# Down projection's last classic part: tokens on the output partitions, with the order of loads, copies and squares changed

## What is computed

```python
def swiglu(h, w_gate_up, w_down):
    gu = h @ w_gate_up
    g, u = gu[..., :D_FF], gu[..., D_FF:]
    return (jax.nn.silu(g) * u) @ w_down
...
        h = h + swiglu(rms_norm(h, g_ffn[l]), w_gate_up[l], w_down[l])
    return rms_norm(h, g_final)
```

## Time and profile before

| | |
|---|---|
| median of 3 runs | 2607.68 us (2606.93 to 2610.78) |
| the profiled execution | 2607.0 us |
| its span, first to last instruction | 2605.2 us |
| mean granted TensorE clock | 0.999 |
| TensorE busy | 2587.1 us, 99% of the span |
| VectorE busy | 2042.0 us, 78% |
| ScalarE busy | 1329.1 us, 51% |
| chain that ended last, by engine | TensorE 98%, VectorE 1% |

### The profile page before, as it was taken

The page is one execution under the profiler, slowest core; times in us unless marked ns, Lnnn a source line. Parts: engine busy times, 40 slices in busy tenths (PEclk is TensorE's granted clock), DMA queues, the critical chain, the costliest instruction groups (busy, mean ns, idle before and its releaser), DMA issues.

```text
span 2605.2 us, 36741 instructions
## 1 busy us (share of the span) xinstructions
PE 2587.1 (99%) x13665; PEld 2228.5 (86%) x13665; DVE 2042.0 (78%) x3366; ACT 1329.1 (51%) x2465; POOL 96.7 (4%) x154
## 2 busy tenths in 40 slices
PE   8999999999999999999999999999999999999998
PEld 7888888888888888888888888888888888888887
DVE  6556876655999974456879999999999998888886
ACT  6335554444555553446565555555555556456453
POOL 0000000000000000000000000000000001001100
PEclk9999999999999999999999999999999999999999
DMA  7332222545544563224444343443443467678664
GB/s 238 95 90 82 80 82 81 194 145 162 154 138 143 168 248 130 89 96 131 162 113 122 118 138 110 118 138 110 119 137 110 120 201 181 134 187 210 129 177 151
DMA packets 391715, 360.02 MB, mean 138 GB/s; under 512 B 11804, under 2 KB 314996, under 8 KB 388980
## 3 DMA queue, kind: packets, MB, share of 16 engines
q1 hardware_dynamic: 373620, 292.67, 37.9%
q0 software_dynamic: 17920, 65.02, 9.0%
HBM read 304.17 MB, written 53.48 MB: 137 GB/s over the span
## 4 chain that ended last, share of the span: by engine, by line
PE 98%; DVE 1%; ACT 0%; DMA 0%; issue 0%; DVEq 0%; ACTq 0%
PE bank L1026 35%; PE bank L1037 18%; PE bank L784 12%; PE bank L785 12%; PE bank L786 12%; PE bank L799 2%; PE bank L801 2%; PE bank L800 2%; PE bank L907 0%; DVE y_out L2710 0%; PE bank L895 0%; PE bank L838 0%; PE bank L1144 0%; PE bank L894 0%; PE bank L921 0%; PE bank L919 0%
## 5 line engine op out<-in xcount | busy, mean ns | idle before, releaser
L2111 DVE TENSOR_TENSOR w_lo<-braw,w_hi 128x512 fp32r<-128x512 f32 x504 | 323.3, 685 | 22.1 <-ACT w_hi L1408 22.1
L1408 ACT ACTIVATE w_hi<-braw 128x512 fp32r<-128x512 f32 x504 | 285.7, 626 | 52.4 <-PE bank L786 19.5
L1838 DVE TENSOR_TENSOR w_lo<-raw,w_hi 128x512 fp32r<-128x512 f32 x224 | 154.3, 691 | 201.4 <-ACT w_hi L1223 200.5
L1223 ACT ACTIVATE w_hi<-raw 128x512 fp32r<-128x512 f32 x224 | 141.5, 632 | 287.5 <-PE bank L786 282.7
L1840 DVE SCALAR_TENSOR_TENSOR w_lo<-raw,par,w_hi 128x512 fp32r<-128x512 f32 x208 | 155.3, 750 | 146.3 <-ACT w_hi L1223 145.2
L2111 DVE TENSOR_TENSOR h_both<-braw,h_both 128x512 fp32r<-128x512 f32 x392 | 251.3, 685 | 2.7 <-ACT h_both L1408 2.5
L1223 ACT ACTIVATE w_hi<-raw,par 128x512 fp32r<-128x512 f32 x208 | 149.4, 721 | 187.0 <-PE bank L786 117.7
L1408 ACT ACTIVATE h_both<-braw 128x512 fp32r<-128x512 f32 x392 | 222.0, 626 | 21.9 <-PE bank L1037 17.5
L784 PE MATMUL bank<-h_both,w_hi 128*128 128x512 f32 x576 | 228.8, 397 | 0.3 <-DVE v_c L1997 0.3
L785 PE MATMUL bank<-h_both,w_hi 128*128 128x512 f32 x576 | 224.9, 390 | 0.0
L786 PE MATMUL bank<-h_both,w_lo 128*128 128x512 f32 x576 | 224.5, 390 | 0.0
(11 more groups left out here) (310 smaller groups left out, 5636.3 us busy)
## 6 DMA issues: line engine op xcount, KB each, us to landing
braw<-in_w_gate_up_dram SPq DMA_DIRECT2D x160, 512.0 KB, 5.0
raw<-in_w_in_dram SPq DMA_DIRECT2D x80, 512.0 KB, 3.7
braw<-in_w_in_dram SPq DMA_DIRECT2D x64, 512.0 KB, 4.8
braw<-in_w_down_dram SPq DMA_DIRECT2D x64, 512.0 KB, 5.9
raw<-in_w_out_dram SPq DMA_DIRECT2D x32, 512.0 KB, 3.8
raw<-in_w_down_dram SPq DMA_DIRECT2D x24, 512.0 KB, 5.4
hidden_spilled<-up_t POOLq DMA_DIRECT2D x44, 256.0 KB, 5.6
raw<-in_w_attn_o_dram SPq DMA_DIRECT2D x16, 512.0 KB, 3.8
```

The costliest lines, as they stand in the source:

```text
L1223: nc.scalar.activation(w_hi[:, s, :], raw[:, n % RAW, (b0 + k) % 2, :], ACT.Copy, scale=sc).then_inc(s_hi, 1)
L1408: nc.scalar.activation(st.slot_hi[s], weights(name, b)[:, 4 * half:4 * half + 4, :], ACT.Copy).then_inc(st.hi, 1)
L1838: nc.vector.tensor_tensor(w_lo[:, s, :], src, w_hi[:, s, :], ALU.subtract).then_inc(s_lo, 1)
L2111: nc.vector.tensor_tensor(st.slot_lo[s], weights(name, b)[:, 4 * half:4 * half + 4, :], st.slot_hi[s], ALU.subtract).then_inc(st.lo, 1)
```

## The change

- In classic 2 the tokens stand on the output partitions: hidden values (128 tokens) are the stationary operand and weights (512 channels) the moving one. There are 16 outputs of 128 tokens by 512 channels, each of 12 matmuls of 128x512. Their order `END` is (token tile, channel group): (0,0) (1,0) (0,1) (1,1) ... (1,3), then token tile 2 with its four groups, then token tile 3.
- The weights of groups 1 to 3 (parts 4 to 15) get places of their own, `end_hi` and `end_lo`, where the block stage's operands lay. ScalarE converts them without waiting for single matmuls, once the block stage's last product has been made.
- The residual is transposed instead of the result: four 128x128 transposes for each output, placed between the products by `END_ROWS`. ScalarE copies them to `y_out`, VectorE adds the products' bank. Six banks hold products, two hold transposes.
- ScalarE squares each piece with its sum along the row in the accumulator; so the column sums on TensorE go. VectorE multiplies each piece by the gain, computes the inverse root once per token tile (four times in all), and scales each piece by it. The last two of the 16 scalings are VectorE's, two of the last tile's ScalarE's.
- All four residual loads are issued behind the last weight load. Copies of pieces come ahead of squares in ScalarE's list.
- Three stores of 1 MB and four of 256 KB take the place of eight of 512 KB.

```diff
+        y_out = at("y_out", 96 * KB, [P, TT, D])
+        end_hi = at("end_hi", 0, [P, 3 * CK, 512], F32R)
+        end_lo = at("end_lo", 24 * KB, [P, 3 * CK, 512], F32R)
...
+        END = [(t, c) for c in range(4) for t in range(2)] + [(t, c) for t in (2, 3) for c in range(4)]
+        END_LAST = {6: 0, 7: 1, 11: 2}
+        END_ROWS = {4: (0,), 5: (1,), 6: (2,), 7: (3,), 8: (4,), 9: (5, 6), 10: (7, 8), 11: (9, 10), 12: (11, 12), 13: (13, 14), 14: (15,)}
+        END_SQUARES = {i: (i - 3,) for i in range(3, 12)} | {12: (9, 10), 13: (11,), 14: (12, 13), 15: (14, 15)}
+        END_GAINS = {i: (i - 4,) for i in range(4, 12)} | {12: (8, 9), 13: (10, 11), 14: (12, 13, 14)}
...
@@ sync: loads @@
+            def residual_load(c):
+                for p in range(2):
+                    sp.wait_ge(s_add[p], 32 * (9 + c))
+                sp.wait_ge(ffn.used, down[1].number("P6" if c < 2 else "P7", DB - 1) + 2)
+                sp.dma_start(acc_end[:, 4 * c:4 * c + 4, :], acc_dram[c]).then_inc(s_ald[c], 16)
...
                 if i == 2:
-                    for c in range(2):
...
                     for p in range(RAW, 8):
                         down_load(i, p)
-                    for c in range(2, 4):
...
+                    for c in range(4):
+                        residual_load(c)
...
@@ sync: stores @@
-            for m in range(2 * TT):
-                t, f = m // 2, slice((m % 2) * (D // 2), (m % 2 + 1) * (D // 2))
-                sp.wait_ge(s_y, 2 * (m + 1))
+            for t in range(TT - 1):
+                sp.wait_ge(s_y, 4 * t + 4)
+                sp.dma_start(out[0, t * P:(t + 1) * P, :], y_out[:, t, :]).then_inc(s_out, 16)
+            for c in (2, 0, 3, 1):
...
@@ tensor @@
+            def end_products(i):
+                t, c = END[i]
...
+                    pe.wait_ge(s_freed, 4 * G_LAST + i - 5)
+                ts = slice(t * P, (t + 1) * P)
+                for k in range(CK):
+                    wait_block(B_DOWN + CK * (8 + c), 0, None, k)
...
+                    pe.matmul(sums[i % 6][:, :], act[:, 0, ts], hi, start=(k == 0), stop=False)
+                    pe.matmul(sums[i % 6][:, :], act[:, 0, ts], lo, start=False, stop=False)
+                    mm = pe.matmul(sums[i % 6][:, :], act[:, 1, ts], hi, start=False, stop=(k == CK - 1))
+                mm.then_inc(s_done, 1)
+
+            def end_rows(i):
+                t, c = END[i]
+                pe.wait_ge(s_ald[c], 16)
...
+                    pe.wait_ge(s_rows, i - 1)
+                for q in range(4):
+                    mm = pe.transpose(rows_[i % 2][:, q * P:(q + 1) * P], acc_end[:, 4 * c + q, t * P:(t + 1) * P], ident[:, :])
+                mm.then_inc(s_fT, 1)
+
+            for i in range(16):
+                end_products(i)
+                for r in END_ROWS.get(i, ()):
+                    end_rows(r)
...
@@ scalar @@
+            for n in range(SPL, 4 * CK):
+                m = B_DOWN + 2 * 4 * CK + n
+                if n == SPL:
+                    act.wait_ge(ffn.used, down[1].halves())
...
+                nc.scalar.activation(end_hi[:, n - SPL, :], raw[:, m // 2 % RAW, m % 2, :], ACT.Copy).then_inc(s_hi, 1)
...
+            def rows_copy(i):
+                act.wait_ge(s_fT, i + 1)
...
+                nc.scalar.activation(y_part(i), end_banks()[1][i % 2][:, :], ACT.Copy).then_inc(s_rows, 1)
+
+            def rows_square(i):
...
+                act.wait_ge(s_freed, 4 * G_LAST + i + 1)
...
+                nc.scalar.activation(tile4[:, i % 2, :], y_part(i), ACT.Square,
+                                     accum_out=ssq[:, 4 * t + c:4 * t + c + 1]).then_inc(s_sqr, 1)
+
+            for i in range(16):
+                rows_copy(i)
+                for n in END_SQUARES.get(i, ()):
+                    rows_square(n)
+                if i in (10, 11, 13):
+                    t = min(i, 12) - 10
+                    root(5 + t, rcol[:, t:t + 1], rtm[:, t:t + 1])
+            root(8, rcol[:, 3:4], rtm[:, 3:4])
+            act.wait_ge(s_rcol, 7)
+            for c in range(2):
+                y = y_out[:, 3, 512 * c:512 * c + 512]
+                nc.scalar.activation(y, y, ACT.Copy, scale=rcol[:, 3:4]).then_inc(s_y3, 1)
...
@@ vector @@
+            def rows_sum(i):
+                dve.wait_ge(s_rows, i + 1)
+                done(G_LAST + i // 4, i % 4)
+                nc.vector.tensor_tensor(y_part(i), y_part(i), end_banks()[0][i % 6][:, :], ALU.add).then_inc(s_freed, 1)
+
+            def rows_gain(i, dst):
...
+                return nc.vector.tensor_tensor(dst, y_part(i), gfin[:, 512 * c:512 * c + 512], ALU.mult)
+
+            def rows_rstd(t):
+                one = slice(t, t + 1)
+                link(nc.vector.tensor_reduce(ssm[:, 0:1], ssq[:, 4 * t:4 * t + 4], mybir.AxisListType.X, ALU.add))
+                rsqrt(5 + t, rcol[:, one], rtm[:, one], rtp[:, one], ssm[:, 0:1]).then_inc(s_rcol, 1)
...
+            def rows_scale(i, src):
...
+                nc.vector.tensor_scalar(y_part(i), src, rcol[:, t:t + 1], None, ALU.mult).then_inc(s_y, 1)
+
+            for i in range(16):
+                rows_sum(i)
+                for n in END_GAINS.get(i, ()):
+                    dve.wait_ge(s_sqr, 2 * KT + n + 1)
+                    link(rows_gain(n, y_part(n)))
+                    if n in END_LAST:
+                        rows_rstd(END_LAST[n])
+                        for m in range(16):
+                            if END[m][0] == END_LAST[n]:
+                                rows_scale(m, y_part(m))
+            rows_gain(15, tile4[:, 3, :])
+            dve.wait_ge(s_sqr, 2 * KT + 16)
+            rows_rstd(3)
+            rows_scale(14, y_part(14))
+            rows_scale(15, tile4[:, 3, :])
```

More of the change, by code:

```diff
@@ L314, in act_tile, with end_weight, end_banks, y_part @@
             return (CK + SK) * (i // CK) + i % CK
+        END = [(t, c) for c in range(4) for t in range(2)] + [(t, c) for t in (2, 3) for c in range(4)]
[3 more added lines that the diff above has]
+        END_GAINS = {i: (i - 4,) for i in range(4, 12)} | {12: (8, 9), 13: (10, 11), 14: (12, 13, 14)}
+        def end_weight(c, k):
+            if c == 0:
+                return w_hi[:, k % SPL, :], w_lo[:, k % SPL, :]
+            return end_hi[:, CK * (c - 1) + k, :], end_lo[:, CK * (c - 1) + k, :]
+        def end_banks():
+            first, second = banks(G_LAST), banks(G_LAST + 1)
+            return [first[0], first[1], first[2], second[2], first[3], second[0]], [second[3], second[1]]
+        def y_part(i):
+            t, c = END[i]
+            return y_out[:, t, 512 * c:512 * c + 512]
         def evicted(n, j):
@@ L1176, in _ @@
             products(ffn)
-            for i in range(3):
+            for i in range(2):
                 for c in range(4):
@@ L1187, in _ @@
                         columns(banks(g), k, CK, act[:, 0, :], act[:, 1, :], wait_bank=free)
-                if i < 2:
[L1189 to L1202, removed]
+                products(down[i])
@@ new lines, in _ @@
+            sums, rows_ = end_banks()
+            first, second = blocks_freed(down[1], 0), blocks_freed(down[1], 1)
+            def end_products(i):
+                t, c = END[i]
+                if i < 6:
+                    ((first, 0), (first, 1), (first, 2), (second, 2), (first, 3), (second, 0))[i][0]((0, 1, 2, 2, 3, 0)[i])
+                else:
+                    pe.wait_ge(s_freed, 4 * G_LAST + i - 5)
+                ts = slice(t * P, (t + 1) * P)
+                for k in range(CK):
+                    wait_block(B_DOWN + CK * (8 + c), 0, None, k)
+                    if i == 0:
+                        pe.wait_ge(s_alo, 2 * CK + k + 1)
+                    act, (hi, lo) = act_place(2 * CK + k), end_weight(c, k)
+                    pe.matmul(sums[i % 6][:, :], act[:, 0, ts], hi, start=(k == 0), stop=False)
+                    pe.matmul(sums[i % 6][:, :], act[:, 0, ts], lo, start=False, stop=False)
+                    mm = pe.matmul(sums[i % 6][:, :], act[:, 1, ts], hi, start=False, stop=(k == CK - 1))
+                mm.then_inc(s_done, 1)
@@ L2671, in _ @@
                         classic_part(1, n)
[L2673 to L2682, removed]
-            for n in range(SPL, 4 * CK):
[L2685 to L2689, removed]
```

80 lines of the change are left out of this document (30 added, 50 removed).

## The result

| | before | after |
|---|---|---|
| median | 2608.12 us (2606.93 to 2610.78, 8 runs) | 2615.62 us (2615.13 to 2616.52, 8 runs) |
| the profiled execution | 2607.0 us | 2616.3 us |
| its span | 2605.2 us | 2614.4 us |
| last stage, its first matmul to the end of the span | 64.05 us | 73.45 us |

The changed kernel is slower: the ratio is 1.0027, interval 1.0018 to 1.0036, which is 7.5 us on the medians. The trace is therefore read against its own 9.4 us of the last stage, and t is counted from that stage's first matmul, 2540.95 here.

A forecast was written before the change was run, and what follows sets the result against it. TensorE, busy 99% of the span, was taken as the bound, with VectorE taking over in the changed tail. The stage's +2.5 us and a residual wait of 1.9 made +4.4 on 2607.7: 2612.1 us, range 2608.8 to 2615.8.

The forecast's parts named there:

- The likeliest case: Last stage: the sum as forecast, residual wait 1.0 to 2.8 us, giving 2611 to 2613.3 us; chance 0.50.
- the third rival: First transposes: a late residual wait of 2.8 us also halves TensorE's clock, losing 1.7; 2614.7 us, chance 0.18.
- The residual's landing: First transposes: the residual, issued behind the last weight load, comes late and makes TensorE wait 1.9 us.
- The early end: Residual load: 0.27 MB/us beside an accumulation, then 0.40 with the gain; landing at 2556.0, a wait of 1.0 us.
- The late end: Residual load: nothing moves until 2551.9, then 2.1 MB at 0.40 MB/us; landing at 2557.8, a wait of 2.8 us.
- The clock: TensorE behind the residual wait: half speed for 3.4 us loses 1.7 us; kept out of the sum, chance 0.18.
- ScalarE's start: Ahead of the pieces: the table load for the root falls where ScalarE is idle, at no cost.
- Sum 9: VectorE's sum of piece 9 starts at t = 38.4 without a residual wait; no gap on VectorE from there.
- VectorE's chain: From sum 9 to the last scalings: VectorE works without gaps and bounds the tail, 20.6 + 3.1 us.
- the fourth rival: VectorE's scalings run at the pace of a sum, 12 x 0.20 us more; 2614.5 us, chance 0.10.
- the fifth: VectorE keeps up and TensorE bounds the stage; 2604.3 us, or 2602.4 with no residual wait, chance 0.05.
- The end: Behind the last scalings: last store issued 1.6 us later, span ending 2.8 us after that, at t = 66.5.

The follow-up runs named there:

- Experiment 2: The changed kernel with twelve useless matmuls on TensorE ahead of its first wait for the residual; 2613.88 us, ratio to before 1.0022.
- experiment 1: The changed kernel with the first two residual quarters loaded ahead of the last four weight loads; 2612.54 us, ratio to before 1.0016.
- experiment 6: As experiment 1, with ScalarE's table load ahead of the pieces, last four weight parts converted behind copy 0, gain awaited at step 4; 2609.99 us, ratio 1.0007.
- experiment 5: As experiment 1, with the gain products of pieces 0 to 14 left out; 2606.6 us, ratio to before 0.9992.
- experiment 7: The changed kernel with three residual quarters first, transposes behind their own product, weights between pieces, roots spread, gain products unlinked; 2603.33 us, ratio to before 0.9982.
- experiment 8: As experiment 7, with the gain products of pieces 0 to 14 left out; 2603.21 us.
- experiment 4: As experiment 1, with gain products not waiting for their own end except where a root follows; 2611.68 us, ratio to before 1.0011.
- experiment 3: The changed kernel with the final gain's broadcast issued only when the first residual quarter has landed; 2620.47 us, ratio to before 1.0050.

## Why the prediction was half right

The range held the time, and the sign was right. The likeliest case was 3.5 us too low; what happened is the third rival, a late residual that also halves the clock, at 2614.7 against 2615.6. That it comes so near, and that the range holds at all, is partly luck. The time lies 0.2 us under the upper end, and the two traces, which the sum is about, are 9.4 us apart in the stage where the medians are 7.5 apart; 9.4 on the prediction's base of 2607.7 would be 2617.1. Both terms of the rival were too small, the wait by 0.7 and the clock by 1.1. (Its chances above 2612.9 also add up to 0.36, not 0.37.) Step by step, against the predicted +4.4 of the stage and the +9.4 measured:

- **The residual's landing: mis-sized, +1.6.** Place and mechanism were right: the first transposes needed it at t = 13.8 (2554.73), and it was issued at 2546.88 for a predicted 2547.0. The wait was 3.51, outside the bounds of 1.0 to 2.8; the failed term is the time of the transfer. The early end had 0.27 MB/us beside an accumulation, and the row has 0.11 MB/us beside POOL's queue until 2553. The late end had the course wrong and the amount right, by luck: nothing until 2551.9 and 0.40 MB/us behind it give 2.1 MB at 2557.1, and SP's queue had in fact moved 0.54 MB by 2553 and 2.17 by 2557.0. So 0.9 of the 1.6 is the middle taken in place of the late end, 0.5 the landing (1.2 us behind 2557.0 for 0.7), and 0.2 the earlier start of this stage. The rule of the Trainium skill (DMA: Bandwidth & Descriptors, section Queues, rings and completion order), which I had set aside because the trace of before showed no hardware packet in 2546 to 2551, is borne out in its first part: both queues moved at once, at 73% and 29% of the engines. The early end that I put beside it was wrong all the same: the two queues moved 1.22 and 0.53 MB in those 5 us. And the row that made me set the rule aside was misread. In before SP issued one load at 2541.66, which landed 3.8 us later, and the next at 2548.20, so until then its queue had nothing to move (SP's timeline in before):

```profile
2541.66 0.38 SPq L639 DMA_DIRECT2D raw<-in_w_down_dram  x1
```

  Only the 3 us from 2548.20 to that load's first packet, at 2551.2, are a delay beside POOL's queue; in after the load issued at 2545.19 had its first packets 2.7 us later. Why either took so long is not shown.
- **The clock: left out of the sum, +2.8.** It stood in the rivals with 0.18 and a price of 1.7. Experiment 2 shows the cause and the price. The size was taken from before, 3.4 us at the lower level; here it was 6.8. The chance was too low too: the bounds of the wait went up to 2.8 and the only row of a wait, 3.50, showed a fall, which should have tied the two together.
- **ScalarE's start: wrong, but covered.** "The table load stays ahead of the pieces, where ScalarE is idle" holds only while the first transposes are late. The conversions wait for the last weights, and the table load stands between them and copy 0. Experiments 1 and 6 price this wait, which the prediction didn't have: 1.9 us between them.
- **Sum 9: right.** Predicted 38.4 without waits, 38.2 in experiment 6; in after 38.4 + 3.5 + 2.8 = 44.7, as measured.
- **VectorE's chain: right, −0.3.** Predicted 23.7 to the last scalings, measured 23.4, without gaps. A scaling takes 0.49 and four take 1.67, a pitch of 0.40, so the fourth rival falls, and experiment 5 excludes the fifth. A root sequence took 1.58 (2588.28 to 2589.86) for 1.64. A linked gain product costs 0.73, as given (0.60 to the product behind sum 9, 2586.23, and 0.73 more where the next waits for its end: three of them take 2.13), and unlinking the seven of the ten products behind sum 9 that no root follows gave 0.87, 0.12 each, since the next operation then starts 0.60 behind.
- **The end: +1.0.** The last store was issued 1.9 us behind the start of the last scalings for 1.6, as four stores take 1.79 of the queue, and the end came 3.5 behind that for 2.8. The first of the four did land sooner than before's larger ones (2.2 us for 2.7), but each one behind it took longer, 2.6, 2.9 and 3.2 us.

Together 4.4 + 1.6 + 2.8 − 0.3 + 1.0 = 9.5, for 9.4 measured. What remains open is why the clock fell for 3.4 us behind before's wait of 3.50 and for 6.8 behind after's of 3.51; no run varies that alone.

As for the change itself: without any new wait it can't be told from before (experiment 6, 1.5 us above it on the medians, with an interval that takes in none; its length is 3.0 more). Before's stage is 44.3 us of products and 19.7 behind them; the change's is 38.2 to sum 9, 23.4 of VectorE behind it and the stores. Its gain appears when that work is spread over the whole stage (experiments 7 and 8).

## What to carry to other kernels

When a tail is moved under a busy engine, ask at what step the engine that now carries it falls behind, and feed it from the first step on: nearly the same operations cost 67.0 us in one order and 60.3 in another (experiments 6 and 7; the links are 0.9 of the difference). Price a new wait of TensorE with the clock in it, and look for the wait that stands just behind it, since removing the first one shows only the difference of the two. A load needed early goes ahead of loads needed late even if the queue seems free, and a one-time wait (the gain) belongs at its first use, not at the head of a list.

## What the runs showed of the hardware

- A longer wait of TensorE did not always mean a lower clock: 1.92 us lowered it once, 2.08, 1.75, 1.56 and 1.53 in other executions did not, 3.50, 3.51 and 6.48 did. Nor did the waits of 1.8 us late in the stage, in five kernels. Each is one execution. The time at the lower level was 3.4 us in two cases (before, experiment 4) and 6.8 in two (after, experiment 3).
- Twelve matmuls without use inside a wait kept the clock up and saved the 2.8 us lost behind it; the stage was 1.9 shorter, as the residual came 0.8 later in that execution.
- Beside accumulating DMAs and a broadcast to all partitions, SP's queue got 29% of the engines and 0.11 MB/us; alone it moved 0.43 MB/us.
- Four stores of 256 KB issued within 1.3 us of each other landed 2.2, 2.6, 2.9 and 3.2 us behind their issue; before's stores of 512 KB, 1.3 us apart, took 2.6 to 2.7 each.
- A table load of ScalarE took 1.28 us between conversions and the first copy.
